# The second pointwise bias of a Conformer block: added to the residual by VectorE instead of by eight one-row matmuls

## The chip, the cores and the metric

The kernel runs on one core of a Trainium2 chip. Its time is device microseconds (us) of one execution; of several executions the median is given. A decoder trunk of two layers is computed in one launch, for 512 tokens of width 1024.

## The reference, cut to what matters

Layer 0 mixes tokens by retention, layer 1 by a Conformer convolution module; each is followed by a mixture-of-experts layer (top group, then two of its eight experts). The change touches the last line of the convolution module and the residual that it is added to:

```python
def conformer_conv_mixer(h, w_pw1, b_pw1, w_dw, b_dw, ln_g, ln_b, w_pw2, b_pw2):
    u = h @ w_pw1 + b_pw1
    a, gate = jnp.split(u, 2, axis=-1)
    u = a * jax.nn.sigmoid(gate)
    z = <causal depthwise convolution, width 31>(u, w_dw) + b_dw
    z = silu(layernorm(z) * ln_g + ln_b)
    return z @ w_pw2 + b_pw2

# layer 1
h = rmsnorm(x, norm_mix_g[1])
x = x + conformer_conv_mixer(h, ...)
h = rmsnorm(x, norm_ffn_g[1])
x = x + hierarchical_moe(h, ...)
return rmsnorm(x, final_norm_g)
```

`b_pw2` is one row of 1024 numbers, the same for all tokens.

## The kernel before

Each engine has its own hand-written instruction stream, and semaphores tie the streams together; nothing is scheduled by a planner. The 512 tokens lie as four tiles of 128 tokens (index `i`); `x[:, i, :]` is the residual, 128 x 1024 for each `i`. PSUM `ps` has eight banks of 128 x 512 float32.

**The order of the program.** Start (loads, rotary tables, first norm), retention with four heads, `turn_x` and `route(0)`, the 32 experts of layer 0, `combine`, a norm and its transposes (`turn_norm(2)`), the first pointwise product in four parts `j`, the depthwise convolution (VectorE takes most channels, TensorE the others), LayerNorm, the second pointwise product in two halves `n` (512 output columns each), `turn_x`, `route(1)`, the 32 experts of layer 1, and the last combine and norm.

**A product** (`product`, L694) runs over eight weight tiles `k` of 128 rows, and for each over four banks `m`. Float32 operands are split into a high and a low part, so that each bank gets three matmuls (`three`, L688). ScalarE makes the high part of a weight tile (`split_hi`, L508), GpSimd the low part (`split_lo`, L428, instruction at L431); four tiles fit ahead. The last matmul of a tile raises `tile_used`, by which the tile's place comes free, and by which SyncE issues further weight loads.

**The place of the change on TensorE.** Behind each half of the second product stand four matmuls, one for each token tile, with one row of contraction: a row of ones times the row `bias_2`, added to the bank as the last part of its accumulation (L908 to L910). Each raises `pw2_mm`, and VectorE then adds the bank to `x` (L1266 to L1270), which raises `x2_added`:

```python
                for i in range(NT):
                    nc.tensor.matmul(ps[:, 4 * n + i, :], const[0:1, C_ONE:C_ONE + P], bias_2[:, n * 512:(n + 1) * 512],
                                     start=False, stop=True).then_inc(pw2_mm, 1)
```

`turn_x` (L677) then transposes `x` into the eight banks by 32 transposes: banks 0 to 3 wait for VectorE's four adds of the first half, banks 4 to 7 for those of the second. ScalarE copies the even banks out (L524), VectorE the odd ones (L937). TensorE goes on with the router product (L746), ScalarE with the sums of squares and roots of the norm (`norm_roots`, L504 and L505), and VectorE with the routing (`route`, L998), at the end of which `cum_ready` releases SyncE's loads of expert weights (L358 to L363).

**The place of the change on VectorE.** In front of the first pointwise product VectorE makes the low part of the normed, transposed tokens (`norm_lo`, L948), clears the padding of the convolution (L1202), and then waits for the gate of the first part (`glu(0)`, L1208).

**The load of the bias.** ScalarE's queue issues four loads at the start, of which the third is `bias_2` (L556). All four raise `par_loaded`, and ScalarE (L563) and VectorE (L1138) wait for all four before they scale the first transposed tokens. SyncE's queue meanwhile loads positions, constants, the four tiles of `x` and the first weights.

**The twin.** `turn_x` and the router product are also run after the retention, at about 453 us of the trace, where the last product goes straight over into the transposes, with no bias matmul between them.

Of the kernel before, what the change touches and what calls it, by code (L numbers as in the profile page):

```python
# [21 lines left out]
ALU = mybir.AluOpType  # L22
# [7 lines left out]
P = 128  # L30
S = 512
D = 1024
NT = S // P
KT = D // P
# [17 lines left out]
NWT = 4  # L52
TILES = 8

C_ID, C_TRI, C_ONE, C_IOTA, C_MOD = 0, 128, 256, 384, 456
# [35 lines left out]
def program(nc, x_in, pos_in, const_in, decay_in, par_in, w_in, w_out, w_pw1, w_pw2, b_pw2,  # L92
            w_router, b_router, w_gu0, w_gu1, w_down, g_final, out):
    with ExitStack() as ctx:
        def sb(name, shape, dt=F32):
            return ctx.enter_context(nc.sbuf_tensor(name, shape, dt))
# [11 lines left out]
        ps = ctx.enter_context(nc.psum_tensor("ps", [P, 8, 512], F32))  # L108
# [3 lines left out]
        x = sb("x", [P, NT, D])  # L112
# [9 lines left out]
        const = sb("const", [P, NCONST])  # L122
        par = sb("par", [P, NPAR])
        wr = sb("wr", [P, NL, KT, NG + NE])
        bias_2 = sb("bias_2", [1, D])
        bias_r = sb("bias_r", [P, NL, NG + NE])
        small = sb("small", [P, 64])
        counting = sb("counting", [P, 2, P], F32R)
# [13 lines left out]
        def over(name, shape, under, words):  # L142
# [74 lines left out]
        par_loaded = sem("par_loaded")  # L217
# [14 lines left out]
        hi_ready, lo_ready, tile_used = sem("hi_ready"), sem("lo_ready"), sem("tile_used")  # L232
# [16 lines left out]
            zh_ready, pw2_mm, x2_added, pad_zero, dve_conv = (  # L249
                sem(n) for n in ("sig_ready", "u_ready", "z_ready", "mean_mm", "centred", "squared", "var_mm",  # L250
                                 "lnroot_ready", "zn_ready", "zh_ready", "pw2_mm", "x2_added", "pad_zero",
                                 "dve_conv"))
# [28 lines left out]
        ret_tiles = HEADS * 4 * TILES  # L281
        pw1_tiles = 4 * TILES
# [214 lines left out]
        def _(act):  # L497
            link = Link(act, act_link)
# [54 lines left out]

            act.dma_start(par[:, :], par_in).then_inc(par_loaded, 16)
            act.dma_start(wr[:, :, :, :], w_router).then_inc(par_loaded, 16)
            act.dma_start(bias_2[:, :], b_pw2).then_inc(par_loaded, 16)  # L556
            act.dma_start(bias_r[:, :, :].rearrange("p l e -> p (l e)"), b_router.partition_broadcast(P)) \
                .then_inc(par_loaded, 16)
            act.wait_ge(pad_zero, 1)
# [107 lines left out]
        def _(pe):  # L667
# [20 lines left out]
            def three(at, lhs, rhs, start, stop):  # L688

                nc.tensor.matmul(at, lhs[0], rhs[0], start=start, stop=False)  # L690
                nc.tensor.matmul(at, lhs[0], rhs[1], start=False, stop=False)  # L691
                return nc.tensor.matmul(at, lhs[1], rhs[0], start=False, stop=stop)  # L692

            def product(number, bank, weights_stand, operand=None, begin=True, last=True, tiles=range(TILES),  # L694
                        split=None, turned=None):

                tokens = operand or (hT_hi, hT_lo)
                for k in tiles:
                    w = (w_hi[:, k % NWT, :], w_lo[:, k % NWT, :])
                    pe.wait_ge(lo_ready, number(k) + 1)
                    if split is not None:
                        pe.wait_ge(hThi_ready, split[0] + k + 1)
                        pe.wait_ge(hTlo_ready, split[0] + max(k + 1, split[1]))
                    if turned is not None:
                        pe.wait_ge(oT_ready, turned + (k + 1))
                        pe.wait_ge(oTlo_ready, turned + (k + 1))  # L710
                    row = k % 4 if operand else k
                    for m in range(4):
                        cols = slice(m * P, (m + 1) * P)
                        start, stop = begin and k == tiles[0], last and k == tiles[-1]
                        if weights_stand:
                            ins = three(ps[:, bank + m, :], [t[:, cols] for t in w], [t[:, row, :] for t in tokens],
                                        start, stop)
                        else:
                            ins = three(ps[:, bank + m, :], [t[:, row, cols] for t in tokens], w, start, stop)
                    ins.then_inc(tile_used, 1)  # L720

            def pick_rows(l, t):
# [102 lines left out]
            with pe.Fori(0, HEADS // 2) as pair:  # L825
                for odd in range(2):
# [16 lines left out]
                    for j in range(NT):  # L843
                        pe.wait_ge(v_ready, 4 * h + (j + 1))
                        for d in range(2):
                            last = nc.tensor.matmul(ps[:, B + j, 0:S - j * P], kT[:, d, j * P:(j + 1) * P],
                                                    qT[:, d, j * P:S], start=(d == 0), stop=(d == 1))
# [4 lines left out]
                    for i in range(NT):  # L852
                        for j in range(i + 1):
                            last = nc.tensor.matmul(ps[:, B + i, :], sT[:, j, i * P:(i + 1) * P], v[:, j, :],
                                                    start=(j == 0), stop=(j == i))
                        last.then_inc(pv_mm, 1)

                    for i in range(NT):
# [3 lines left out]
                        for f in range(NT):  # L862
                            last = nc.tensor.transpose(ps[:, A + f, i * P:(i + 1) * P], sg[:, i, f * P:(f + 1) * P],
                                                       ident)
# [3 lines left out]
                    for n, at in enumerate((B, A)):  # L868
                        if n:
                            pe.wait_ge(oTlo_ready, 4 * h + 4)  # L870
                        product(tile(3), at, False, operand=(oT_hi, oT_lo), tiles=range(4 * n, 4 * n + 4),
                                turned=(4 * h if n == 0 else None))
# [14 lines left out]
            for n, (c, k) in enumerate(pe_taps):  # L887
                if n == len(PE_CHANNELS) * WIDTH:
# [3 lines left out]
                                 start=(k == 0 or k == WIDTH - SHARED_TAPS and c == SHARED),  # L892
                                 stop=(k == WIDTH - 1)).then_inc(diag_used, 1)

            parts = ((z_sum, z_summed, 4), (z[:, 3, :], zpe_ready, 2), (z[:, 6, :], z_ready, 5), (z[:, 7, :], z_ready, 6))
            for n, (part, ready, count) in enumerate(parts):
                pe.wait_ge(ready, count)
                last = nc.tensor.matmul(ps[:, 2, :], ones, part, start=(n == 0), stop=(n == len(parts) - 1))
            last.then_inc(mean_mm, 1)
            for c in range(KT):  # L900
                pe.wait_ge(squared, c + 1)
                last = nc.tensor.matmul(ps[:, 3, :], ones, z_squares[:, c, :], start=(c == 0), stop=(c == KT - 1))
            last.then_inc(var_mm, 1)
            pe.wait_ge(u_ready, KT)
            for n in range(2):
                product(lambda k: ret_tiles + pw1_tiles + n * TILES + k, 4 * n, False, last=False,
                        split=(2 * KT, 0))
                for i in range(NT):  # L908
                    nc.tensor.matmul(ps[:, 4 * n + i, :], const[0:1, C_ONE:C_ONE + P], bias_2[:, n * 512:(n + 1) * 512],
                                     start=False, stop=True).then_inc(pw2_mm, 1)  # L910
            turn_x(x2_added, 2 * NT)
            route(1)
            experts(1)
# [3 lines left out]
        def _(dve):  # L917
            link = Link(dve, dve_link)
            V = nc.vector
# [24 lines left out]
            def norm_lo(n, m, gain):  # L944

                for k in range(KT):
                    dve.wait_ge(hThi_ready, KT * m + k + 1)
                    V.scalar_tensor_tensor(out=hT_lo[:, k, :], in0=ps[:, k, :], scalar=par[:, gain + k:gain + k + 1],  # L948
                                           in1=hT_hi[:, k, :].bitcast(F32), op0=ALU.mult, op1=ALU.subtract) \
                        .then_inc(hTlo_ready, 1)  # L950
# [178 lines left out]
            for n, part in enumerate(TURN):  # L1129
                ins = V.scalar_tensor_tensor(out=ang, in0=turns, scalar=-part, in1=ang, op0=ALU.mult, op1=ALU.add)  # L1130
# [68 lines left out]

            norm_lo(2, 1, G_MIX + KT)
            link.done(V.memset(uT[:, :, 0:PAD], 0.0))  # L1202

            def glu(j):
# [60 lines left out]
                    scale_z(k + 2)  # L1265
            for n in range(2):  # L1266
                for i in range(NT):
                    dve.wait_ge(pw2_mm, 4 * n + i + 1)
                    V.tensor_tensor(x[:, i, n * 512:(n + 1) * 512], x[:, i, n * 512:(n + 1) * 512],
                                    ps[:, 4 * n + i, :], ALU.add).then_inc(x2_added, 1)  # L1270
            turned_x(3)
# [74 lines left out]
```

## Time and profile before

| | |
|---|---|
| median of 3 runs | 1786.35 us (1784.78 to 1788.58) |
| the profiled execution | 1786.88 us, of which 1785.0 us are the span of the trace |
| TensorE busy | 1471.5 us (82%), mean granted clock 0.934 |
| VectorE, ScalarE, GpSimd busy | 522.5, 486.3, 337.2 us |
| DMA moved | 473.19 MB, mean 265 GB/s |

### The profile page before, as it was taken

Reading aid. Unit: us, or ns where it says so; the run is one execution under the profiler, and the core shown is the slowest. Engines: PE = TensorE matmul, PEld = TensorE weight load, DVE = VectorE, ACT = ScalarE, POOL = GpSimd, SP = SyncE. Lnnn points to the kernel's source line nnn. Section 1 sums busy time; section 2 is a strip of 40 time slices with the busy share of each in tenths; the row PEclk is TensorE's granted clock in tenths of the full one; section 3 lists DMA queues with packets and bytes.
Section 4 is the critical chain, followed back from the end, with each engine's and each line's share of the span. In section 5 each row is a group of like instructions: output and inputs, shape, how many; then the busy total and the mean of one; then the engine's idle time right before and its main releaser. Section 6 shows DMA issues by size and latency. Waiting matters only on the chain. (4 is left out here: it accounts for less than half of the span.)

```text
span 1785.0 us, 37105 instructions
## 1 busy us (share of the span) xinstructions
PE 1471.5 (82%) x15156; PEld 936.2 (52%) x15157; DVE 522.5 (29%) x1245; ACT 486.3 (27%) x875; POOL 337.2 (19%) x294
## 2 busy tenths in 40 slices
PE   5999999999786889867785899869788878679883
PEld 4878678786443445434353785337344444345442
DVE  3222111212521112111123399961412111112124
ACT  4232422323321222211122324341322122112222
POOL 2424244342000111100011452012010001001100
PEclk8999999999798999999997899979799899999997
DMA  8222122121599999999998121004499999999985
GB/s 283 96 93 94 48 95 95 47 95 53 192 428 429 427 429 427 429 428 429 429 409 288 47 95 47 0 1 164 180 376 414 406 430 423 429 427 428 415 361 212
DMA packets 65156, 473.19 MB, mean 265 GB/s; under 512 B 6509, under 2 KB 23101, under 8 KB 39506
## 3 DMA queue, kind: packets, MB, share of 16 engines
q1 hardware_dynamic: 60064, 463.55, 63.4%
q0 software_dynamic: 4608, 8.41, 1.2%
q8 instruction: 38, 0.62, 0.1%
q10 hardware_dynamic: 434, 0.51, 0.1%
q14 instruction: 12, 0.10, 0.0%
HBM read 461.94 MB, written 14.68 MB: 267 GB/s over the span
## 5 line engine op out<-in xcount | busy, mean ns | idle before, releaser
L787 PE MATMUL ps<-ring,hgT 128*32 128x256 f32 x6016 | 385.3, 409 | 147.2 <-DMA ring<-w_gu 122.7
L787 PEld LDWEIGHTS ps<-ring,hgT 128*32 128x32 f32 x6016 | 202.5, 116 | 318.0 <-DMA ring<-w_gu 147.8
L431 POOL TENSOR_TENSOR w_lo<-ring,w_hi 128x512 fp32r<-128x512 f32 x176 | 233.0, 1326 | 415.1 <-ACT w_hi L511 415.1
L450 POOL DMA_INDIRECT y_dram<-area_c,idx_s x96 | 94.3, 982 | 788.6 <-ACT area_c L547 768.9
L511 ACT CAST w_hi<-ring 128x512 fp32r<-128x512 f32 x176 | 109.1, 625 | 367.1 <-PE ps L692 366.7
L730 PE MATMUL ps<-area_a,block_rows 128*32 128x256 f32 x3136 | 201.3, 400 | 8.9 <-DVE block_rows L976 8.9
L1098 DVE TENSOR_TENSOR a_e<-sg_e,ps 128x128 f32<-128x128 f32 x94 | 27.1, 288 | 613.3 <-ACT sg_e L542 613.3
L803 PE MATMUL ps<-ring,aT_e 128*32 128x256 f32 x2752 | 166.3, 382 | 23.6 <-DMA ring<-w_down 10.7
L730 PEld LDWEIGHTS ps<-area_a,block_rows 128*32 128x32 f32 x3136 | 110.3, 117 | 85.0 <-issue 26.6
L1237 DVE SCALAR_TENSOR_TENSOR area_c<-area_b,par,area_c 128x512 f32<-128x512 f32 x168 | 135.6, 878 | 1.1
L690 PE MATMUL ps<-w_hi,hT_hi 128*128 128x512 f32 x320 | 126.7, 396 | 7.2 <-DVE hT_lo L1262 7.2
L542 ACT ACTIVATE sg_e<-ps 128x128 f32<-128x128 f32 x94 | 26.2, 278 | 382.0 <-PE ps L787 382.0
L803 PEld LDWEIGHTS ps<-ring,aT_e 128*32 128x32 f32 x2752 | 83.0, 109 | 86.1 <-ACT aT_e L544 19.4
L691 PE MATMUL ps<-w_lo,hT_hi 128*128 128x512 f32 x320 | 126.2, 394 | 0.0
L692 PE MATMUL ps<-w_hi,hT_lo 128*128 128x512 f32 x320 | 125.8, 393 | 0.0
L542 ACT ACT_TABLE_LOAD x94 | 120.6, 1283 | 12.3 <-DVE cum L1045 10.7
L690 PE MATMUL ps<-hT_hi,w_hi 128*128 128x512 f32 x256 | 102.1, 399 | 13.6 <-POOL w_lo L431 12.6
L691 PE MATMUL ps<-hT_lo,w_hi 128*128 128x512 f32 x256 | 101.5, 397 | 0.0
L692 PE MATMUL ps<-hT_hi,w_lo 128*128 128x512 f32 x256 | 101.4, 396 | 0.0
L547 ACT COPY area_c<-ps 128x256 f32 x94 | 35.1, 373 | 216.7 <-PE ps L803 216.7
L984 DVE TENSOR_TENSOR hgT<-ps,par 128x128 f32<-128x128 f32 x192 | 46.9, 287 | 154.9 <-PE ps L739 154.9
L690 PEld LDWEIGHTS ps<-w_hi,hT_hi 128*128 128x128 f32 x320 | 61.0, 191 | 21.6 <-issue 8.8
(183 smaller groups left out, 1473.6 us busy)
## 6 DMA issues: line engine op xcount, KB each, us to landing
ring<-w_gu SPq DMA_DIRECT2D x128, 2048.0 KB
ring<-w_down SPq DMA_DIRECT2D x58, 2048.0 KB
ring<-w_in SPq DMA_DIRECT2D x8, 2048.0 KB
ring<-w_in SPq DMA_DIRECT2D x8, 1024.0 KB
ring<-w_out SPq DMA_DIRECT2D x4, 2048.0 KB
ring<-w_pw SPq DMA_DIRECT2D x8, 1024.0 KB
hT<-w_down SPq DMA_DIRECT2D x2, 2048.0 KB, 7.7
area_c<-w_down SPq DMA_DIRECT2D x2, 2048.0 KB, 8.0
```

The lines of the kernel that those rows point to most:

```text
L431: nc.gpsimd.tensor_tensor(w_lo[:, place, :], ring[:, s, at:at + 512], w_hi[:, place, :].bitcast(F32), ALU.subtract).then_inc(lo_ready, 1)
L450: pool.indirect_dma_start(y_dram[l], bass.IndirectOffsetOnAxis(ap=idx_s[:, b:b + 1].bitcast(U32), axis=0), y_out[:, b, :], None, bounds_ch ...
L511: nc.scalar.copy(w_hi[:, place, :], ring[:, s, at:at + 512]).then_inc(hi_ready, 1)
L542: nc.scalar.activation(sg_e[:, :], ps[:, 2, 0:P], ACT.Silu).then_inc(silu_ready[l], 1)
L690: nc.tensor.matmul(at, lhs[0], rhs[0], start=start, stop=False)
L691: nc.tensor.matmul(at, lhs[0], rhs[1], start=False, stop=False)
L692: return nc.tensor.matmul(at, lhs[1], rhs[0], start=False, stop=stop)
L730: last = nc.tensor.matmul(ps[32 * g:32 * g + 32, 6, 0:QW], block_rows[:, i, :], xn[:, i, g * QW:(g + 1) * QW], start=(i == 0), stop=(i == ...
L787: last = nc.tensor.matmul(ps[32 * g:32 * g + 32, 2, 0:256], hgT[:, n * (KT // 2) + k, :], gate_up[n][:, k, :, g * P:(g + 1) * P], start=(n ...
L803: last = nc.tensor.matmul(ps[32 * g:32 * g + 32, 4, 0:256], aT_e[:, k * BLK:(k + 1) * BLK], down[:, k, g * 256:(g + 1) * 256], start=(k == ...
L984: ins = V.tensor_tensor(hgT[:, :, :].rearrange("p (q c) s -> p c q s", c=2)[:, c], ps[:, 1, c * P:(c + 1) * P].rearrange("p (q s) -> p q s ...
L1237: ins = V.scalar_tensor_tensor(out=z[:, c, :], in0=uT[:, c, k:k + S], scalar=tap, in1=z[:, c, :], op0=ALU.mult, op1=ALU.add)
```

## The change

The eight bias matmuls go away. `bias_2` is loaded to all 128 partitions (128 x 1024 instead of 1 x 1024), and VectorE adds it to `x` by four instructions of 128 x 1024, between `norm_lo` and the clearing of the padding; by then the norm of `x` has been computed. `pw2_mm` is now raised by the last matmul of the banks 0, 1 and 2 in a half's last tile; for the fourth bank VectorE waits on `tile_used`, which that bank's last matmul raises.

```diff
-        bias_2 = sb("bias_2", [1, D])
+        bias_2 = sb("bias_2", [P, D])
...
-            act.dma_start(bias_2[:, :], b_pw2).then_inc(par_loaded, 16)
+            act.dma_start(bias_2[:, :], b_pw2.partition_broadcast(P)).then_inc(par_loaded, 16)
...
             def product(number, bank, weights_stand, operand=None, begin=True, last=True, tiles=range(TILES),
-                        split=None, turned=None):
+                        split=None, turned=None, done=None):
...
+                        if done is not None and k == tiles[-1] and m < 3:
+                            ins.then_inc(done, 1)
                     ins.then_inc(tile_used, 1)
...
             for n in range(2):
-                product(lambda k: ret_tiles + pw1_tiles + n * TILES + k, 4 * n, False, last=False,
-                        split=(2 * KT, 0))
-                for i in range(NT):
-                    nc.tensor.matmul(ps[:, 4 * n + i, :], const[0:1, C_ONE:C_ONE + P], bias_2[:, n * 512:(n + 1) * 512],
-                                     start=False, stop=True).then_inc(pw2_mm, 1)
+                product(lambda k: ret_tiles + pw1_tiles + n * TILES + k, 4 * n, False, split=(2 * KT, 0),
+                        done=pw2_mm)
             turn_x(x2_added, 2 * NT)
...
             norm_lo(2, 1, G_MIX + KT)
+            for i in range(NT):
+                link.sent(V.tensor_tensor(x[:, i, :], x[:, i, :], bias_2[:, :], ALU.add))
             link.done(V.memset(uT[:, :, 0:PAD], 0.0))
...
                 for i in range(NT):
-                    dve.wait_ge(pw2_mm, 4 * n + i + 1)
+                    if i < 3:
+                        dve.wait_ge(pw2_mm, 3 * n + i + 1)
+                    else:
+                        dve.wait_ge(tile_used, NWT + ret_tiles + pw1_tiles + (n + 1) * TILES)
```

On TensorE, from the last two banks of the second half to the routing (`L685` is `turn_x`, the next line the router product), before:

```order
L690 MATMUL ps<-w_hi,hT_hi 128x512
L691 MATMUL ps<-w_lo,hT_hi 128x512
L692 MATMUL ps<-w_hi,hT_lo 128x512
L909 MATMUL ps<-bias,const 128x512 x4
L685 MATMUL ps<-const,x 128x128 x32
L746 MATMUL ps<-hT,wr 36x512 x8
L751 MATMUL ps<-const,area_b 128x36 x4
```

and with the change (lines are numbered two higher here):

```order
L690 MATMUL ps<-w_hi,hT_hi 128x512
L691 MATMUL ps<-w_lo,hT_hi 128x512
L692 MATMUL ps<-w_hi,hT_lo 128x512
L685 MATMUL ps<-const,x 128x128 x32
L748 MATMUL ps<-hT,wr 36x512 x8
L753 MATMUL ps<-const,area_b 128x36 x4
```

The four bias matmuls between product and transposes are gone; behind the first half, between the two products, the same four go.

On VectorE, in front of the first pointwise product and up to the first taps of the convolution, before:

```order
L948 SCALAR_TENSOR_TENSOR hT_lo<-ps,par,hT_hi 128x512 x8
L1202 MEMSET area_b 128x8x30
L1208 SCALAR_TENSOR_TENSOR area_b<-ps,par,area_c 128x512 x2
L1235 TENSOR_SCALAR area_c<-area_b,par 128x512 x2
L1237 SCALAR_TENSOR_TENSOR area_c<-area_b,par,area_c 128x512 x22
```

and with the change:

```order
L947 SCALAR_TENSOR_TENSOR hT_lo<-ps,par,hT_hi 128x512 x8
L1202 TENSOR_TENSOR x<-x,bias 128x1024 x4
L1203 MEMSET area_b 128x8x30
L1209 SCALAR_TENSOR_TENSOR area_b<-ps,par,area_c 128x512 x2
L1236 TENSOR_SCALAR area_c<-area_b,par 128x512 x2
L1238 SCALAR_TENSOR_TENSOR area_c<-area_b,par,area_c 128x512 x22
```

Four adds stand ahead of the clearing; nothing else on VectorE moves.

On ScalarE's queue, the four loads at the start of the program:

```order
 L554 DMA par<-par_in 128x336
 L555 DMA wr<-w_router 128x576
-L556 DMA bias<-b_pw 1x1024
+L556 DMA bias<-b_pw 128x1024
 L557 DMA bias_r<-b_router 128x72
 L504 ACT_TABLE_LOAD
```

The third load is 128 times as large; the order is the same.

## Rows read from the trace of the kernel before

**Rows 1.** Timeline of TensorE around the bias matmuls of the first half: start us, us, what.
```profile
1212.89 0.39 PE L692 MATMUL ps<-w_hi,hT_lo 128*128 128x512 f32 x1
1213.20 3.69 PE L909 MATMUL ps<-bias,const 1*128 1x512 f32 x8
1216.83 0.50 PE L690 MATMUL ps<-w_hi,hT_hi 128*128 128x512 f32 x1
```

**Rows 2.** Windows: stretch, its length, busy time of PE (instructions), PEclk, DMA share, GB/s.
```profile
1213.20:1216.80 3.60, 3.60 (x9) 1.00 0.02 5
1217.60:1221.00 3.40, 3.40 (x10) 0.52 0.00 0
```

**Rows 3.** Timeline of TensorE from the second half's end to the router product.
```profile
1235.80 0.39 PE L691 MATMUL ps<-w_lo,hT_hi 128*128 128x512 f32 x1
...
1240.11 0.39 PE L692 MATMUL ps<-w_hi,hT_lo 128*128 128x512 f32 x1
1240.42 3.69 PE L909 MATMUL ps<-bias,const 1*128 1x512 f32 x8
1244.05 5.38 PE L685 MATMUL ps<-const,x 128*128 128x128 f32 x32
1249.36 7.06 PE L746 MATMUL ps<-hT,wr 128*36 128x512 f32 x16
```

**Rows 4.** Windows of all engines: stretch, length, busy PE, PEld, DVE, ACT, POOL, then PEclk, DMA share, GB/s.
```profile
1245.00:1248.50 3.50, 3.50 (x19) 3.50 (x18) 1.39 (x2) 1.51 (x3) 0.00 (x0) 0.51 1.00 426
453.20:457.40 4.20, 3.92 (x33) 3.38 (x31) 4.01 (x7) 2.03 (x4) 0.00 (x0) 1.00 0.75 242
1253.00:1267.00 14.00, 5.98 (x21) 3.02 (x19) 7.11 (x34) 9.27 (x16) 0.00 (x0) 0.70 0.00 0
1300.00:1700.00 400.00, 324.10 (x5168) 177.07 (x5156) 72.36 (x280) 86.13 (x157) 39.19 (x44) 0.95 1.00 422
6.00:8.00 2.00, 0.00 (x0) 0.00 (x0) 0.45 (x2) 0.00 (x0) 0.00 (x0) 1.00 1.00 382
```

**Rows 5.** Timeline of TensorE at the twin, after the retention.
```profile
453.15 2.47 PE L685 MATMUL ps<-const,x 128*128 128x128 f32 x19
455.89 1.64 PE L685 MATMUL ps<-const,x 128*128 128x128 f32 x13 [0.27 <-DVE x L1191]
457.46 7.06 PE L746 MATMUL ps<-hT,wr 128*36 128x512 f32 x16
```

**Rows 6.** Timeline of VectorE and SyncE from the second half's end to the expert loads.
```profile
1241.58 0.69 DVE L1269 TENSOR_TENSOR x<-x,ps 128x512 f32<-128x512 f32 x1 [23.96 <-PE ps L909]
1256.42 0.18 DVE L942 RECIPROCAL small<-small 128x4 f32<-128x4 f32 x1 [6.26 <-ACT small L505]
1267.64 0.33 SPq L361 DMA_DIRECT2D hT<-w_down  x1
```

**Rows 7.** Timeline where the adds are put; and a VectorE instruction of the adds' shape.
```profile
992.41 4.97 POOL L431 TENSOR_TENSOR w_lo<-ring,w_hi 128x512 fp32r<-128x512 f32 x4 [28.92 <-ACT w_hi L511]
993.73 0.79 PE L690 MATMUL ps<-hT_hi,w_hi 128*128 128x512 f32 x1 [5.20 <-POOL w_lo L431]
1021.15 1.41 DVE L1208 SCALAR_TENSOR_TENSOR area_b<-ps,par,area_c 128x512 f32<-128x512 f32 x2 [27.73 <-ACT area_c L625]
1275.98 1.22 DVE L1070 TENSOR_TENSOR slot_hot_r<-const,area_b 128x1024 fp32r<-128x1024 f32 x1
```

**Rows 8.** GpSimd's groups while VectorE runs the taps (1020 to 1100 us).
```profile
L431 POOL TENSOR_TENSOR w_lo<-ring,w_hi 128x512 fp32r<-128x512 f32 x25 | 38.2, 1527 | 29.8 <-ACT w_hi L511 29.8
```

**Rows 9.** DMA queue q10 (ScalarE's) from 6 to 8 us; an issue's count, KB, us to landing.
```profile
q10 hardware_dynamic: 152, 0.13, 19.6%
...
trig<-g_final SPq DMA_DIRECT2D x1, 512.0 KB, 11.7
```

**Rows 10.** Timeline of the start of the program.
```profile
8.95 1.28 ACT L504 ACT_TABLE_LOAD   x1 [8.95 <-DMA x<-x_in]
20.07 4.74 ACT L517 ACTIVATE hT_hi<-ps,par 128x512 fp32r<-128x512 f32 x8 [0.59 <-PE ps L673]
```

## The prediction

> **What bounds the kernel now.** I read the page first: TensorE is busy 82% of the span, far more than any other engine. That average hides stages with different limits, so the timeline around the bias matmuls comes next. The reader should see that they stand in the open: the last matmul of the first half starts at 1212.89, the bias instructions at 1213.20, and the next product cannot start before 1216.83 [rows 1]; the same happens behind the second half, 1240.11, 1240.42 and 1244.05 [rows 3]. TensorE has no gap there, every engine behind waits for it: VectorE had stood still for 23.96 us before its first add of the second half [rows 6].
>
> Then the windows, for the clock. During the first bias group it is 1.00, full 2.4 GHz, and soon after, from 1217.6 to 1221.0, 0.52, so nearly all of it at 1.2 GHz [rows 2]. Behind the second group, from 1245.0 to 1248.5, in the transposes, it is 0.51 [rows 4]. TensorE never stood still there. So each bias group is followed by a dip, two of two.
>
> Last, what is behind. Transposes, norm, routing and then the expert loads follow one another: the expert loads start at 1267.64 [rows 6], and from 1253 to 1267 DMA moves nothing [rows 4]. From 1300 to 1700 DMA is busy 1.00 of the time at 422 GB/s and TensorE 324.10 of 400 us [rows 4], so the expert stage is bound by the loads, but its stream of loads starts only when the routing releases it. Time won in front of the routing should therefore move the whole rest to the left, though that rest is not TensorE's.
>
> **Removed, behind the first half.** From the last product matmul to the next product's first are 1216.83 - 1212.89 = 3.94 us [rows 1]. Without the bias group this is one step from matmul to matmul. From 1235.80 to 1240.11, at full clock, there are 19 steps, so one is 0.227 us [rows 3]. Gain 3.7 us.
>
> **The dip behind it.** The second half's 96 matmuls start at 1216.83 [rows 1] and the last of them at 1240.11 [rows 3]: 23.28 us for 95 steps. At 0.227 us, 95 steps take 21.55 us. The dip costs 1.7 us. Products that follow a product with nothing between them show no such dip, so I count it as gone.
>
> **Removed, behind the second half.** 1244.05 - 1240.11 = 3.94 us [rows 3], less one step, again 3.7 us.
>
> **The transposes.** They take 1249.36 - 1244.05 = 5.31 us now [rows 3]. At the twin, where no bias matmul stands in front, the clock stays at 1.00 [rows 4] and they take 457.46 - 453.15 = 4.31 us, of which 0.27 us are a wait for VectorE's adds [rows 5]. Here the adds start bank by bank: the first may start nine matmuls (2.0 us) before the product ends, four of 0.69 us [rows 6] are done about 1 us after it, and bank 4 is transposed 2 us after it. So I take 4.04 us, without the wait, and keep 4.31 as the other end. Gain 1.3 us (1.0 to 1.3). VectorE's wait for the fourth bank now goes to `tile_used`, raised by a matmul that the old form waited for too; behind it on VectorE only the copies of odd banks are queued, and they wait for transposes anyway.
>
> Is all of that on the path? Two chains leave the transposes: the router product, ending at 1249.36 + 7.06 = 1256.42 [rows 3], and ScalarE's roots, which release VectorE at 1256.42 [rows 6]. They arrive together, and both start from the transposes, so neither holds the other back when both move. The removed sum is 3.7 + 1.7 + 3.7 + 1.3 = 10.4 us.
>
> **Added on VectorE.** Four adds of 128 x 1024. An instruction of that shape takes 1.22 us [rows 7], so 4.9 us. They are hidden: between the clearing of the padding and the gate VectorE stands still for 27.73 us [rows 7]. That cover would have to shrink below 4.9 us to cost anything. Their place is not empty for GpSimd, though: it makes four low parts there from 992.41 on, 4.97 us, and TensorE's first matmul at 993.73 waits for the first of them [rows 7]. Beside VectorE's taps that instruction takes 1527 ns on average [rows 8] against 4.97 / 4 = 1.24 us here. The adds would begin where VectorE now clears the padding, 0.3 us before 1021.15 - 27.73 = 993.42 [rows 7]. The first low part is half done by then, so I take 0.1 us. The upper bound is one whole add in front of it, 1.2 us; the lower bound is nothing, as each later part has a tile's time to spare.
>
> This is the place where a rule speaks against the change. The Trainium skill, "SBUF — State Buffer", section "Who interferes with whom", says that a VectorE instruction with two SBUF inputs and a GpSimd instruction that reads SBUF exclude each other, and whichever issues second waits for the other's end. The stretched 1527 ns agrees with it in sign and is less than a full wait; by the rule the low parts would alternate with the adds at about 2.5 us each, still inside a tile's time at the low clock, and the sum would stay.
>
> **Added at the start.** The bias load grows from 4 to 512 KB, and the first link of the start is the arrival of `x`, which holds ScalarE until 8.95 [rows 10]. From 6 to 8 us the DMA engines are busy 1.00 of the time at 382 GB/s [rows 4], and ScalarE's queue moves its last 0.13 MB [rows 9]. With the change its queue has 0.5 MB more to send, by my estimate from about 7 us on, when the first tile of `x` still has about 1 us to go and then gets about half of the bandwidth. Upper bound: all of it goes first, 0.5 MB / 382 GB/s = 1.3 us; lower bound: none, if it comes late. I take 0.8 us. From there ScalarE's squares and roots go on without slack up to the transposes: at 20.07 it has waited 0.59 us for them [rows 10]. Nothing later gives the shift back, since the retention follows TensorE. The wait for all four small loads comes at 20.07 - 0.59 = 19.5 us, when the broadcast should long be in.
>
> **The sum.** -10.4 + 0.1 + 0.8 = -9.5 us. Against the profiled execution's own 1786.88 us this gives 1777.4. That execution lies 0.5 us above the median of the three runs, so against the median 1786.35 it gives **1776.9, rounded to 1777 us**.
>
> **Rivals.**
>
> *The dips are not the bias's.* Then removing the groups gives 7.4 us, and the dips come in the same places or close by: -7.4 + 0.9 = -6.5, 1779.9 us. For it: TensorE was busy without a gap in the groups, 3.60 of 3.60 us [rows 2]. Against it: two of two, and none at the twin, where the transposes and the router product run at 1.00 [rows 4]. The Trainium skill has this rival as its rule: "TensorE: Matmul & The Clock Gate", Part 1, ties the clock to how busy TensorE has been, and by it a group that leaves no gap lowers nothing. Chance 0.12.
>
> *The load stream hides it.* If the expert stage began its stream at a time of its own, the gain would vanish in it and the time would be 1786.35 + 0 to 0.9, about 1787. For it: DMA share 1.00 from 1300 to 1700 [rows 4]. Against it: no traffic at all from 1253 to 1267, and the first load at 1267.64 [rows 4, 6], released by the routing. Chance 0.04.
>
> *The broadcast is late, and the kernel is slower.* 128 copies are read from one row of 4 KB in HBM. ScalarE and VectorE wait for all four small loads in front of 20.07 [rows 10]. The only load of this shape in the trace, `g_final`, took 11.7 us from issue to landing behind three large loads [rows 9]; here, issued in the first microseconds, it would be in time. It starts to cost when it lands after about 20 us, and outweighs the 10.4 us only when it lands after 30; to be slower by over 3.6 us it must land after about 34, three times the row. It would then give 1790 or more. Chance 0.03.
>
> *The change does not do what it says.* The order of instructions shows the eight matmuls gone and VectorE's adds in, so nothing is left for this.
>
> **How the numbers follow.** Forecast 0.81, rivals 0.12, 0.04 and 0.03. About 0.2%, 3.6 us, is what a measurement can tell from no change; the runs before lie 3.8 us apart. The forecast's own bounds are 1776.9 with +0.5 - 0.8 at the start, +1.1 on GpSimd and +0.3 in the transposes, so 1776 to 1779. A shifted start can also move the stretches at the low clock after a stop; one such dip was worth 1.7 us, and I allow one either way, with 1 us for the spread of the runs. That gives 1773.5 to 1781.5, which also takes in the first rival. Faster: 0.81 + 0.12 = 0.93. Same 0.04. Slower 0.03.
>
> **What would show it right or wrong.** In the profile of the changed kernel: the two products of the second pointwise follow each other at steps of 0.227 us with the clock at 1.00; the transposes start one step after the last matmul and take about 4.0 us at 1.00; from the first product matmul of the first half to the first expert load there are 10.4 us less. At the start ScalarE's first work begins at about 9.7 instead of 8.95, and everything up to the expert stage of layer 0 is shifted by that. VectorE has four adds of about 1.2 us at 994, with over 20 us of idle time behind them. The forecast is wrong if a dip stays in the second half or in the transposes, if the adds delay the first product's start by more than 1 us, or if the distance from the first expert load of layer 1 to the end grows by what was won.

## The result, and the profile after

| | before | changed |
|---|---|---|
| median of 5 runs, same chip | 1785.69 us (1784.78 to 1788.58) | 1775.88 us (1774.35 to 1777.78) |
| ratio, 95% interval | | 0.9944 (0.9929 to 0.9958) |
| span of the profiled execution | 1785.0 us | 1775.0 us |

Faster by 10.0 us by the ratio (7.5 to 12.7 by its interval; the medians lie 9.8 us apart), where 1777 against 1786.35 us, 9.4 us, was forecast.

TensorE's timeline of the changed kernel around the place where the first group stood, and from the end of the second half to the router product (start, us, what), answers to [rows 1, 3]:

```profile
1215.00 0.39 PE L692 MATMUL ps<-w_hi,hT_lo 128*128 128x512 f32 x1
1215.22 0.39 PE L690 MATMUL ps<-w_hi,hT_hi 128*128 128x512 f32 x1
...
1235.40 0.39 PE L692 MATMUL ps<-w_hi,hT_lo 128*128 128x512 f32 x1
1235.63 3.65 PE L685 MATMUL ps<-const,x 128*128 128x128 f32 x32
1239.21 7.06 PE L748 MATMUL ps<-hT,wr 128*36 128x512 f32 x16
```

The products go on at a step of 0.23 us; the transposes begin one step after the last matmul and take 1239.21 - 1235.63 = 3.58 us, not 5.31. The windows of all engines (stretch, length, busy PE, PEld, DVE, ACT, POOL, then PEclk, DMA share, GB/s) answer to [rows 2, 4]:

```profile
1216.00:1235.00 19.00, 19.00 (x86) 15.72 (x85) 1.22 (x2) 2.49 (x4) 5.18 (x5) 1.00 0.31 110
1235.10:1239.10 4.00, 4.00 (x36) 3.78 (x34) 3.45 (x6) 1.98 (x4) 0.00 (x0) 1.00 0.61 168
1290.00:1690.00 400.00, 327.11 (x5168) 178.29 (x5160) 72.30 (x280) 85.96 (x157) 39.22 (x44) 0.94 1.00 423
```

The clock is 1.00 in the second half's product and in the transposes: both dips are gone. The expert stage is as full of DMA as before, and it too has moved to the left. VectorE and SyncE behind it, as [rows 6]:

```profile
1233.78 2.73 DVE L1273 TENSOR_TENSOR x<-x,ps 128x512 f32<-128x512 f32 x4 [19.03 <-PE ps L692]
1246.25 0.18 DVE L941 RECIPROCAL small<-small 128x4 f32<-128x4 f32 x1 [6.24 <-ACT small L505]
1257.46 0.33 SPq L361 DMA_DIRECT2D hT<-w_down  x1
```

VectorE's adds start 1.85 us before the transposes and run without a pause. Where the time went, from marks in the two timelines:

| stretch | before | changed | difference |
|---|---|---|---|
| start to the first product matmul | 28.16 | 28.84 | +0.68 |
| to the first matmul of the first pointwise | 965.57 | 966.02 | +0.45 |
| to the first matmul of the second pointwise | 195.21 | 194.92 | -0.29 |
| to the transposes | 55.11 | 45.85 | -9.26 |
| the transposes | 5.31 | 3.58 | -1.73 |
| to the first expert load of layer 1 | 18.28 | 18.25 | -0.03 |
| to the end | 517.36 | 517.54 | +0.18 |
| span | 1785.0 | 1775.0 | -10.0 |

The place of the adds, timeline of three engines, as [rows 7]:

```profile
993.53 11.44 POOL L431 TENSOR_TENSOR w_lo<-ring,w_hi 128x512 fp32r<-128x512 f32 x6 [28.92 <-ACT w_hi L511]
994.21 8.36 DVE L1202 TENSOR_TENSOR x<-x,bias 128x1024 f32<-128x1024 f32 x4
994.86 0.79 PE L690 MATMUL ps<-hT_hi,w_hi 128*128 128x512 f32 x1 [5.19 <-POOL w_lo L431]
1022.02 1.41 DVE L1209 SCALAR_TENSOR_TENSOR area_b<-ps,par,area_c 128x512 f32<-128x512 f32 x2 [19.19 <-ACT area_c L625]
```

Four adds take 8.36 us, not 4.9, and the six low parts that GpSimd makes meanwhile 11.44 us. Not all of the six stand beside an add, so the durations of single instructions say more (ns, least/median/most):

```profile
L1202 DVE TENSOR_TENSOR x<-x,bias x4: 1678/2296/2316, 994.2 to 1000.2; 128x1024 f32<-128x1024 f32 x4
L431 POOL TENSOR_TENSOR w_lo<-ring,w_hi x6: 1269/2255/2276, 993.5 to 1003.7; 128x512 fp32r<-128x512 f32 x6
```

An add takes 2.3 us instead of 1.22 and a low part beside it 2.26 instead of 1.28. Both are covered: VectorE stands still for 19.19 us afterwards, and TensorE starts 1.33 us after the first low part's start, as before (1.32).

The start, as [rows 10], and the load itself (issue's count, KB, us to landing):

```profile
10.18 1.28 ACT L504 ACT_TABLE_LOAD   x1 [10.18 <-DMA x<-x_in]
20.78 4.73 ACT L517 ACTIVATE hT_hi<-ps,par 128x512 fp32r<-128x512 f32 x8
...
bias<-b_pw ACTq DMA_DIRECT2D x1, 512.0 KB, 8.8
```

The first tile of `x` is 1.23 us later, the first product matmul 0.68 (28.84 for 28.16).

### The profile page after: what moved, and what is told of

It is laid out like the page before. It is cut to its first block and busy times, and to the rows that moved or that the text cites. A ratio compares the mean times of both kernels' runs of the same rounds, so it can differ in the third digit from the quotient of the medians.

```text
span 1775.0 us, 37077 instructions
## 1 busy us (share of the span) xinstructions
PE 1464.5 (83%) x15140; PEld 933.1 (53%) x15141; DVE 529.9 (30%) x1249; ACT 485.3 (27%) x875; POOL 340.5 (19%) x294
## 5 line engine op out<-in xcount | busy, mean ns | idle before, releaser
L431 POOL TENSOR_TENSOR w_lo<-ring,w_hi 128x512 fp32r<-128x512 f32 x176 | 236.8, 1347 | 406.1 <-ACT w_hi L511 406.1
L732 PE MATMUL ps<-area_a,block_rows 128*32 128x256 f32 x3136 | 205.2, 406 | 8.9 <-DVE block_rows L975 8.9
```

The lines of the kernel that those rows point to most:

```text
L431: nc.gpsimd.tensor_tensor(w_lo[:, place, :], ring[:, s, at:at + 512], w_hi[:, place, :].bitcast(F32), ALU.subtract).then_inc(lo_ready, 1)
L732: last = nc.tensor.matmul(ps[32 * g:32 * g + 32, 6, 0:QW], block_rows[:, i, :], xn[:, i, g * QW:(g + 1) * QW], start=(i == 0), stop=(i == ...
```

## The experiments

Two theories of the dips: **A**, the one-row matmuls let the clock fall; **B**, the clock follows busy time or a rhythm of its own, and the dips fell behind the groups by chance. Beside them: what the load costs at the start, what each group is worth, and what covers the adds. Each kernel was timed beside the kernel before; differences between kernels are read as ratios to that one.

### e1_load_only: the load alone

```diff
-        bias_2 = sb("bias_2", [1, D])
+        bias_2 = sb("bias_2", [P, D])
...
-            act.dma_start(bias_2[:, :], b_pw2).then_inc(par_loaded, 16)
+            act.dma_start(bias_2[:, :], b_pw2.partition_broadcast(P)).then_inc(par_loaded, 16)
...
-  bias_2[:, n * 512:(n + 1) * 512]
+  bias_2[0:1, n * 512:(n + 1) * 512]
```

> The kernel before with only the load of the bias made 128 times as large; the eight one-row matmuls stay. My theory (the load pushes back the first tile of x and nothing gives that back): ScalarE's first work starts near 10.2 us as in the changed kernel, not at 8.95, TensorE's first product matmul near 28.8 instead of 28.16, and the time is 0.7 to 1.0 us above the kernel before. Rival (other slack absorbs the shift before the experts): start shifted, but the first expert load of layer 1 stays at 1267.6 and the time is the same. Both dips of the clock stay, in both theories.

Measured: ratio 1.0010 (1.0000 to 1.0019), 0 to 3.4 us slower. ScalarE's first work starts at 10.14, the first product matmul at 28.62. But the first expert load of layer 1 stands at 1266.56, before the 1267.64 of the kernel before, so the 0.46 us are lost in what the stages between vary by (e4_late_load below shows what varies there). The shift of the start is shown, its price in the whole time only as small. Both dips are there, at 0.50 (stretch, length, busy PE, PEclk, DMA share, GB/s):

```profile
1216.50:1219.50 3.00, 3.00 (x8) 0.50 0.00 0
1243.80:1247.00 3.20, 3.20 (x17) 0.50 1.02 435
```

### e2_rows128: the same matmuls with 128 rows

Against e1_load_only:

```diff
-  const[0:1, C_ONE:C_ONE + P], bias_2[0:1, n * 512:(n + 1) * 512]
+  ident, bias_2[:, n * 512:(n + 1) * 512]
```

> As the kernel before, but each of the eight bias matmuls contracts 128 rows (identity times the bias on all 128 partitions, the same sum) instead of one. Their duration should stay at 3.6 us a group, since they have as many columns. Theory A (a matmul that uses one row of the array lets the clock fall): no dip in the second half's product nor in the transposes; the product matmuls of the second half start 95 steps of 0.227 apart and the transposes take about 4.0 to 4.3 us; the time is 3 us below the kernel before, less 0.8 for the larger load, so about 2 below. Theory B (the clock follows how busy TensorE is, or a phase of its own): dips of about 3.4 us at 0.5 stay behind both groups and the time is 0.8 us above the kernel before.

Measured: ratio 0.9989 (0.9981 to 0.9998), 0.4 to 3.4 us faster. TensorE's windows and timeline:

```profile
1212.10:1215.50 3.40, 3.40 (x10) 1.00 0.02 5
1216.00:1222.00 6.00, 6.00 (x28) 1.00 0.00 0
1237.30:1240.60 3.30, 3.30 (x9) 1.00 0.65 184
1240.70:1244.20 3.50, 3.50 (x33) 1.00 1.00 431
```

```profile
1237.25 3.59 PE L909 MATMUL ps<-bias,const 128*128 128x512 f32 x8
1240.68 3.66 PE L685 MATMUL ps<-const,x 128*128 128x128 f32 x32
1244.27 7.06 PE L746 MATMUL ps<-hT,wr 128*36 128x512 f32 x16
```

Eight matmul instructions of the same number of columns stand in both places, TensorE is as busy as before, and no dip follows either group. Theory A holds, B falls; e8_rows32 below shows how far A goes. From the second group to the transposes are 3.43 us, against 3.63 with one row, and the transposes take 3.59 us. From the second pointwise's first matmul (1188.13) to the first expert load (1262.53) are 74.40 us against 78.70 before.

### e3_first_half and e7_second_half: one group at a time

In e3_first_half, against the changed kernel (e7_second_half mirrors it):

```diff
-                link.sent(V.tensor_tensor(x[:, i, :], x[:, i, :], bias_2[:, :], ALU.add))
+                link.sent(V.tensor_tensor(x[:, i, 0:512], x[:, i, 0:512], bias_2[:, 0:512], ALU.add))
...
+                if n != 0:
+                    for i in range(NT):
+                        nc.tensor.matmul(ps[:, 4 * n + i, :], const[0:1, C_ONE:C_ONE + P],
+                                         bias_2[0:1, n * 512:(n + 1) * 512],
+                                         start=False, stop=True).then_inc(pw2_mm, 1)
```

> The change for the first half of the columns alone: VectorE adds 512 columns, the first group of bias matmuls is gone, the second stays. Theory: the first group was worth 3.7 us plus a dip of 1.7 us, so from the first product matmul of the first half to the first expert load 5.4 us go, and the time is 5.4 - 0.8 = about 4.6 us below the kernel before; the dip in the transposes stays. Rival (the two dips are one effect of the clock's own phase): the dip in the second half's product stays or appears elsewhere, 3.7 us go.

> The change for the second half of the columns alone: the first group of bias matmuls stays, the second is gone. Theory: from the first product matmul of the second pointwise to the first expert load, 3.7 us for the group and 1.7 us for the transposes at full clock go (5.31 to 3.6 us, as the changed kernel shows), 5.4 us; the dip in the second half's product stays, at 1.7 us. The time is 4.6 us below the kernel before. Rival (one dip displaced is another gained): the transposes take more than 4.5 us although nothing with one row stands in front of them.

Measured: e3_first_half ratio 0.9983 (0.9974 to 0.9992), 1.4 to 4.6 us faster; e7_second_half 0.9966 (0.9956 to 0.9977), 4.1 to 7.9 us. Windows of TensorE, first those of e3_first_half:

```profile
1212.00:1236.00 24.00, 24.00 (x107) 1.00 0.29 104
1240.80:1243.50 2.70, 2.70 (x14) 0.50 1.00 431
```

and of e7_second_half:

```profile
1218.50:1221.50 3.00, 3.00 (x9) 0.50 0.00 0
1241.10:1244.60 3.50, 3.50 (x33) 1.00 0.70 197
```

Each dip comes with its group and goes with it; without their group the transposes take 3.59 us in e7_second_half, with it 4.97 in e3_first_half. There the clock fell about 0.6 us before the group's end, and the group itself took 3.92 us instead of 3.63; behind the other one-row groups the dip began 0.7 to 1.0 us after the end. From the second pointwise's first matmul to the first expert load are 1263.97 - 1190.75 = 73.22 us in the one and 1262.93 - 1189.81 = 73.12 in the other, against 78.70: each group with its dip is worth 5.5 to 5.6 us, and the two together are the 11.0 us of the changed kernel. In the whole time the 4.6 us expected stand inside e7_second_half's interval and at the very edge of e3_first_half's. The latter's trace lost 1.1 us in the stretch ahead, from the first to the second pointwise (196.35 us against 195.21), where the change has only its adds. What varies there is the clock. All engines' window of e3_first_half in the convolution, and the same one of the changed kernel:

```profile
1174.40:1178.00 3.60, 3.60 (x5) 1.53 (x6) 3.30 (x6) 3.60 (x7) 0.00 (x0) 0.50 0.02 5
1174.40:1178.00 3.60, 2.55 (x6) 1.24 (x7) 3.60 (x7) 3.24 (x6) 0.00 (x0) 1.00 0.02 5
```

Summed over the stretch, e3_first_half's TensorE has 29.1 us at half the clock and that of the kernel before 24.5. The traces of e9_adds_first and e10_adds_apart, which leave this place alone, have the same longer dip there (196.06 and 196.15 us for the stretch), so it isn't the work of this edit.

### e8_rows32: a quarter of the rows

Against e1_load_only:

```diff
-  const[0:1, C_ONE:C_ONE + P], bias_2[0:1, n * 512:(n + 1) * 512]
+  const[0:32, C_ONE:C_ONE + P], bias_2[0:32, n * 512:(n + 1) * 512]
...
+            link.sent(V.tensor_scalar(bias_2[:, :], bias_2[:, :], 1.0 / 32, None, ALU.mult))
```

Measured: ratio 1.0004 (0.9994 to 1.0014), the same time. Windows of TensorE behind the two groups:

```profile
1217.50:1221.00 3.50, 3.50 (x10) 0.55 0.00 0
...
1243.70:1247.30 3.60, 3.60 (x33) 1.00 1.02 437
```

A dip behind the first group and none behind the second: neither of the two expectations. So it isn't the form with one partition alone, and with 32 rows it isn't certain to happen. What decides between the two groups was not tried, and how many rows are enough to be safe stays open between 32 and 128.

### e4_late_load, e5_after_again, e6_late_again: the load out of the way

```diff
-            act.dma_start(bias_2[:, :], b_pw2.partition_broadcast(P)).then_inc(par_loaded, 16)
...
             load_rows(3, w_out, 0, DV)
+            sp.dma_start(bias_2[:, :], b_pw2.partition_broadcast(P)).then_inc(bias_loaded, 16)
...
+            dve.wait_ge(bias_loaded, 16)
```

> The changed kernel with the bias loaded by SyncE's queue behind the first weights instead of by ScalarE's at the start, with a semaphore of its own. Theory: the start is that of the kernel before again (ScalarE at 8.95, first product matmul at 28.2), the rest as in the changed kernel: 0.7 to 1.0 us below the changed kernel. Rival (the shift of the start isn't what separates the two): same time as the changed kernel. Bandwidth taken from the retention's weight loads should cost nothing, as these are waited for nowhere.

> The changed kernel once more, as the yardstick of this group on its chip: 9 to 10 us below the kernel before, and again no dip behind either half of the second product.

> The kernel of e4_late_load once more, beside the changed kernel on one chip. Theory: 0.8 us below it, since the first product matmul starts 0.8 us earlier. Rival, from the trace of e4_late_load (first product matmul at 28.00, yet the transposes after the retention at 454.74, later than the changed kernel's 453.48): stages in front of the experts vary by 1 us and more from one execution to the next, and the 0.8 us are lost in that: medians within 1.5 us, of either sign.

Measured: e4_late_load 0.9954 (0.9941 to 0.9967). On another chip, side by side, the changed kernel 0.9936 (0.9921 to 0.9952) and the late load 0.9946 (0.9932 to 0.9961). The changed kernel's repetition is thus 11.4 us below the kernel before (9 to 10 were expected, inside the interval), and its trace again has the clock at 1.00 behind both halves. In e4_late_load's trace the first product matmul starts at 28.00, so the start is repaired:

```profile
28.00 0.80 PE L691 MATMUL ps<-hT_hi,w_hi 128*128 128x512 f32 x1 [8.19 <-POOL w_lo L433]
```

yet the transposes after the retention stand at 454.74, later than the changed kernel's 453.48, and the time is no better. In e5_after_again they stand at 454.64, from a first matmul at 28.70: two executions of the same kernel differ by 1.3 us in the retention (424.64 and 425.94 us). Here too the clock differs. All engines' window of e5_after_again in the retention, and the same one in the first trace of the changed kernel:

```profile
114.50:117.50 3.00, 3.00 (x8) 2.32 (x8) 0.55 (x1) 0.00 (x0) 0.00 (x0) 0.50 0.00 0
114.50:117.50 3.00, 3.00 (x15) 2.44 (x14) 1.38 (x3) 0.62 (x2) 0.00 (x0) 1.00 0.00 0
```

In both, TensorE had stood still for 0.78 and 1.57 us shortly before, for the same operands. The clock fell after it in one execution and not in the other. Summed over the retention, TensorE has 7.5 us at half the clock in e8_rows32, 8.5 in the first trace of the changed kernel, 10.4 in e5_after_again and 13.5 in e4_late_load, and the retention takes 424.04, 424.64, 425.94 and 426.74 us.

So the theory, 0.8 us below the changed kernel, is not borne out: side by side the late load is 1.8 us slower by the ratios, with overlapping intervals. That is also more than the 1.5 us of the rival, whose main point stands: the stages in front of the experts vary by more than the 0.8 us. Whether the moved load itself brings on further dips in the retention, one trace can't tell.

### e9_adds_first and e10_adds_apart: the cover of the adds

e9_adds_first moves the four adds in front of `norm_lo(2, 1, G_MIX + KT)`. e10_adds_apart puts them behind the clearing, each with

```diff
+                dve.wait_ge(lo_ready, ret_tiles + NWT + 1 + i)
```

> The changed kernel with the four adds in front of the low parts of the tokens (norm_lo) instead of behind them, so that their cover is gone: the first product waits for norm_lo. GpSimd's first low part is made from about 992.4 on and could meet the last adds. Theory (the adds are free only by their place): the first product matmul of the first pointwise comes later by the adds' own 4.9 us (1.22 each with no GpSimd instruction beside them), less the wait of 1.4 us that VectorE has there for ScalarE, so 3.5 us; the time is 3 to 5 us above the changed kernel. Rival (the slow adds of 2.1 us each are a property of the instruction, not of GpSimd beside it): they take 8.4 us here too and the time is 7 us above the changed kernel.

> The changed kernel with each add waiting for a low part of the fifth to eighth weight tile, so that VectorE and GpSimd take turns instead of meeting. Theory (they exclude each other on the port): each add takes 1.2 us and each low part 1.28 again, instead of 2.1 and up to 2.3 us, and the time is that of the changed kernel, since nothing waited for either: same within 1.5 us. Rival (the meeting did delay something): 1 to 2 us below the changed kernel.

Measured, on one chip: e9_adds_first 0.9950 (0.9937 to 0.9962), e10_adds_apart 0.9931 (0.9919 to 0.9944). VectorE and GpSimd in e10_adds_apart:

```profile
999.27 1.28 POOL L431 TENSOR_TENSOR w_lo<-ring,w_hi 128x512 fp32r<-128x512 f32 x1 [1.54 <-ACT w_hi L511]
1000.66 1.23 DVE L1204 TENSOR_TENSOR x<-x,bias 128x1024 f32<-128x1024 f32 x1 [6.87 <-POOL w_lo L431]
1002.00 1.28 POOL L431 TENSOR_TENSOR w_lo<-ring,w_hi 128x512 fp32r<-128x512 f32 x1 [1.45 <-ACT w_hi L511]
```

and VectorE in e9_adds_first:

```profile
987.11 4.62 DVE L1201 TENSOR_TENSOR x<-x,bias 128x1024 f32<-128x1024 f32 x4
991.65 5.35 DVE L947 SCALAR_TENSOR_TENSOR hT_lo<-ps,par,hT_hi 128x512 fp32r<-128x512 f32 x8
```

An add alone takes 1.23 us and a low part 1.28; side by side they take 2.3 and 2.26. So the meeting with GpSimd is shown as the cause of the 8.36 us. That nobody waited for it the trace of the changed kernel shows (19.19 us of idle time behind the adds, TensorE's first matmul as before); the time agrees, but neither kernel was timed beside the changed one, and the ratios 0.9931 here and 0.9936 and 0.9944 there can't tell 2 us. My expectation for e9_adds_first missed, the rival too (its adds take 4.62 us): `norm_lo` ends 3 us later than in the changed kernel against the same mark, but TensorE's first matmul comes 27.04 us after the rows of layer 0 are fetched (967.48 to 994.52), against 26.95 in the changed kernel. It needs only the first four of eight low parts of the tokens, and waits for the weights' first low part until then anyway; the cover was deeper than I had read it. The median nevertheless lies above e10_adds_apart's by 2.4 us, with overlapping runs; that is unclear. By the ratio to the kernel before it is 1.1 to 2.5 us above the changed kernel's two measurements, not the 3 to 5 expected.

### e11_retention_banks: the same release, in the retention

```diff
-                                turned=(4 * h if n == 0 else None))
+                                turned=(4 * h if n == 0 else None), done=ret_mm)
...
-                        if i == 0:
+                        if i < 3:
+                            dve.wait_ge(ret_mm, 6 * h + (3 * n + i + 1))
+                        else:
                             dve.wait_ge(tile_used, 4 * TILES * h + (3 * TILES + 4 * (n + 1) + NWT))
```

> The changed kernel, and in the retention VectorE's adds to x are released bank by bank in the same way (the last tile's matmuls of banks 0, 1 and 2 raise a semaphore of their own, tile_used releases the fourth) instead of all four by tile_used. The transposes after the retention wait 1.0 us for these adds now and should then take 3.6 us instead of 4.31, 0.7 us less; the next head's product waits for the same adds and may gain up to 0.3 us a head. Expected: 1 to 2 us below the changed kernel, which is at the edge of what the timing can tell; the trace shows the transposes at 3.6 us or not. Rival: the head's end is bound elsewhere and the transposes just begin their wait earlier: same time, transposes still over 4.2 us.

Measured: 0.9933 (0.9918 to 0.9948), beside 0.9931 of e10_adds_apart on the same chip: no difference in time. In its trace the transposes after the retention take 457.71 - 454.12 = 3.59 us instead of 4.31, without a wait:

```profile
454.12 3.65 PE L686 MATMUL ps<-const,x 128*128 128x128 f32 x32
457.71 1.48 PE L749 MATMUL ps<-hT,wr 128*36 128x512 f32 x3
```

The 0.7 us are won there and are below what the timing resolves. The 0.3 us a head don't show: the retention takes 424.90 us, between the 424.64 and 425.94 of the changed kernel. No version is shown to be faster than the changed kernel; e10_adds_apart and e11_retention_banks were not timed beside it.

## Why the prediction was right

**The groups in the open.** Right. Up to the transposes 9.26 us went, against 3.7 + 1.7 + 3.7 = 9.1 forecast.

**The dips.** Right, and the rival with 0.12, "the dips are not the bias's", falls for the one-row groups: in e2_rows128 TensorE is as busy as before in both places and its clock stays at 1.00. By the rule of the Trainium skill cited in the prediction ("TensorE: Matmul & The Clock Gate", Part 1), busy time alone should have kept the clock up behind the one-row groups as well; the trace disagrees, with 0.52 and 0.51 behind groups that left no gap. All six one-row groups of the traces (before, e1, e3, e7) have their dip, both groups of 128 rows have none, and of the two of 32 rows one has. In the six traces without any group (changed, e4, e5, e9, e10, e11) the clock is 1.00 in both places. Dips of the same length occur elsewhere, in some executions and not in others, as in the windows of e5_after_again above; that one follows stops of TensorE, which these groups don't have.

**The transposes.** Right in kind, undersized: 1.73 us, not 1.3. The step that failed is "they take 4.31 us, of which 0.27 us are a wait". The row of the matmuls shows only a part of one wait. TensorE waits first with the weight loads, one of which stands in front of each transpose, and their rows at the twin, in the kernel before, show two waits:

```profile
455.29 0.14 PEld L685 LDWEIGHTS ps<-const,x 128*128 128x128 f32 x1 [0.25 <-DVE x L1191]
455.89 1.40 PEld L685 LDWEIGHTS ps<-const,x 128*128 128x128 f32 x13 [0.46 <-DVE x L1191]
```

These are 0.71 us, of which the 0.27 us of [rows 5] are the visible end of the second; the first lies inside the row that joins 19 transposes. Taken off, the twin gives 4.31 - 0.71 = 3.6 us instead of 4.04, which is what the changed kernel (3.58) and e11_retention_banks (3.59) show. The gain of 1.73 us is the price of the dip alone, the same 1.7 us that the prediction had worked out for the product.

**All of it on the path.** Right: from the router product's start to the first expert load, and from there to the end, nothing changed by more than 0.2 us. The rival of the load stream falls with that.

**The adds.** Hidden, as forecast, with 19.19 us left of 27.73. But their size was wrong by 1.7 times: "an instruction of that shape takes 1.22 us" was read where GpSimd stood still. The rule that I cited against it, from "SBUF — State Buffer", was the better price: low parts alternating with the adds at 2.5 us, where 2.26 were measured at the median, and 1.28 when kept apart. I had set it aside because taps stretched low parts to only 1527 ns [rows 8]; a tap is shorter than an add (0.74 us against 1.22, medians), and so is the wait behind it.

**The start.** 0.68 us against 0.8, by two errors that nearly cancel. The tile of `x` came 1.23 us late, near the upper bound of 1.3, since the load's queue took 0.41 MB from 6 to 8 us, about half of the 0.85 MB moved. "Without slack up to the transposes" was wrong: VectorE's first scaling of `x` took 1.14 us before, beside GpSimd, and 0.75 us when it came later, which gave back 0.4 us: TensorE's transposes of it start at 15.37 instead of 14.61. On ScalarE's own path the 0.59 us of waiting [rows 10] took up the rest. These are VectorE's two rows, of the kernel before

```profile
13.32 1.14 DVE L927 TENSOR_SCALAR area_a<-x,small 128x1024 f32<-128x1024 f32 x1
```

and of the changed one:

```profile
14.46 0.75 DVE L926 TENSOR_SCALAR area_a<-x,small 128x1024 f32<-128x1024 f32 x1
```

**The late broadcast**, the slower rival, falls: it landed 8.8 us after its issue at 1.65, at 10.5. The small load behind it in the queue landed last, at 12.5 (issued at 2.13, 10.4 us), and ScalarE needs all four only at 20.78.

**The sum.** Local gain 11.0 us instead of 10.4, start +0.7 instead of +0.8, nothing at the adds, and +0.3 net (+0.45, -0.29, +0.18) in stretches where the change does nothing or only has its adds: 10.0 us. That the total came within 1 us of the forecast is in part luck: stretches like these differ by 1 us and more between executions of one kernel, and the errors in the transposes and in these stretches have opposite signs.

## What to carry to other kernels

A small operation on the busiest engine costs its own time only if nothing follows from it; here eight matmuls of one row cost 7.4 us themselves and another 3.5 us in the clock behind them, so read the granted clock behind a group as well as within it. A broadcast that all tokens share is nearly free on an engine with a 20 us gap, but check which engine its instructions meet in that gap (here they took 2.3 us instead of 1.22) and what its larger load stands in front of. And when a twin elsewhere in the trace gives the price, look up all of its waits, those of the weight loads too, not only the one that its merged row shows.

## What the runs showed of the hardware that I had not expected

- Eight matmul instructions of one row, with no gap before or behind, bring on about 3.4 us at half the clock, six times of six; eight of 128 rows with the same columns don't, twice of two, and with 32 rows it came once and once not. A group of eight also takes 3.43 us with 128 rows and 3.63 us with one or with 32.
- VectorE's add of two SBUF operands and GpSimd's subtraction stretch each other to 2.3 and 2.26 us (medians), from 1.23 and 1.28, when they run at the same time.
- The retention of one and the same kernel took 424.64 and 425.94 us in two executions, with 8.5 and 10.4 us at half the clock, so that a change of under 1 us at the start could not be followed to the end.
